# Weight sums in nine float32 tiles, GpSimd's sums in another order, sums of x split in three steps

## The chip, the cores and the metric

One core of a Trainium2 chip. The metric is the device time of one launch in microseconds. The program has five engines: TensorE (PE, matmuls), VectorE (DVE), ScalarE (ACT), GpSimd (POOL) and SyncE (SP), which only issues DMAs here.

## The reference

Two blocks of two layers each over 512 tokens of 1024 features in float32. The change lies in the feed-forward part of the second block, run twice:

```python
def squared_relu_mlp(x, w1, w2):
    h = jnp.square(jax.nn.relu(jnp.einsum('bsd,df->bsf', x, w1)))
    return jnp.einsum('bsf,fd->bsd', h, w2)

def second_block(x, mem, ...):
    for l in range(DEPTH):
        ...
        ff = squared_relu_mlp(x, w_ff1[l], w_ff2[l])
        x = layer_norm(ALPHA * x + ff, ln3_g[l], ln3_b[l])
    return x
```

w1 has 4096 columns (32 tiles of 128), w2 has 1024 (8 tiles). Everything ahead of it (attention, recurrence, gated feed-forward, memory attention) is computed as well and isn't touched.

## The kernel before, in words

A float32 matmul is made of three on float32r parts: each weight tile is split by ScalarE into a high part (`split_hi`, L1330) and by VectorE into the rest (`split_lo`, L1949), and TensorE adds high x high, low x high and high x low.

**Groups.** The 32 hidden tiles go in four groups of eight. The first group (f0 = 0) is an ordinary product. The other three (f0 = 8, 16, 24) use a scheme of Strassen's kind: two hidden tiles by the two halves of the 1024 inputs and the two halves of the 512 tokens make a pair, and a pair takes seven half-size products, the *forms*, in place of eight. A group has four pairs, 28 forms; form m = 7p + j is the j-th of pair p. Each has 12 matmuls of 256 columns on TensorE (`tensor_forms`, L1297 to L1302). After each group come the eight w_ff2 tiles w0 to w7, each 24 matmuls of 512 columns. So a layer runs: group 0, w0 to w7, then three times (28 forms, w0 to w7). With two layers there are six *form stages*, numbered 1 to 6 here.

**Weight sums.** The seven forms of a pair need sums of blocks of w_ff1. They are made by DMAs: SP loads a block of 256 KB into a half of a staging tile (*base load*, L2966), GpSimd issues further DMAs that add a block to it (L2885). A pair has four *chains*: chain 0 (forms 0 and, after one sum, 5), chain 1 (forms 1 and, after one, 4), chain 2 (form 2) and chain 3 (after two sums form 3, after the third form 6). *Sum (p,c,s)* is the s-th sum of chain c of pair p; a group has 20. A sum may only be issued once the chain's contents so far have been split for their form, and (p,3,s) once (p,3,s-1) has landed.

**Staging.** Three staging tiles of float32 hold all loaded weights. In a form stage they are six halves (`CHAIN_HALF`), so pair p+1's chains wait for pair p's splits. w0, w1 and w2 of the group can be loaded only after the splits of forms 27, 25 and 23 (`FORMS_STAGING`).

**Orders.** Every engine runs its list in order. ScalarE in `forms`: at each step m it waits for form m, at j = 0 copies `first` (L1870, needed by form j = 2 of that pair), at j = 1 `third` (needed by j = 5), at j = 2 the first result, then splits the high part of form m+6 (`split_form_hi`, L1337), and at j = 6 does relu, square and the high part of the hidden tile. VectorE follows with the low parts (`split_form_lo`, L1957) and the combinations (L2683 to L2701; L2687 is `inner2`, needed by j = 6). The splits of forms 0 and 1 come after w5's product, of 2 and 3 after w6's, of 4 and 5 after w7's. The split buffers (three) let form m+6 be split when form m is done.

GpSimd's order of a group before is (0,3,1), (0,3,2), then for p = 0 to 3: (p,0,1), (p,1,1), (p+1,3,1), (p,3,3), (p+1,3,2).

**Sums of x.** The forms also need sums of blocks of x (`sums`, L2661 to L2666, in temps 6 to 13), split into high parts by ScalarE (L1916) and low parts by VectorE (`sums_low`, L2672), the latter four at a time after the first four w_ff2 tiles of group 0.

## Time and profile before

| | us |
|---|---|
| median of 3 runs (2941.24 to 2949.04) | 2948.06 |
| the profiled execution | 2945.99 |
| its span, first to last instruction | 2944.3 |
| TensorE busy in the span | 2790.1 (95%) |
| VectorE, ScalarE, GpSimd busy | 1769.5, 1317.9, 508.7 |

The six form stages begin at 1793.28, 1892.83, 1997.48, 2619.05, 2725.42 and 2824.82 us of the span. Busy time of TensorE is modelled from pipelined matmuls; what counts is how far apart they start: 0.12 us for the forms' matmuls where nothing waits. In a view of windows the columns are: the stretch, its length in us, busy time (and instructions) of PE, PEld, DVE, ACT and POOL, the granted TensorE clock as a share of full speed, the busy share of the DMA engines, GB/s. An idle time in brackets ends when the named releaser's last semaphore event came; where that engine had waited itself, one reads on there.

### The profile page before, as it was taken

The page shows a single profiled execution, that of the slowest core. Times are in us where ns is not written, and L with a number is a line of the kernel's source. Part 1 is how long each engine was busy: PE and PEld are TensorE (multiplying, and loading weights), DVE is VectorE, ACT ScalarE, POOL GpSimd, SP SyncE. Part 2 cuts the span into 40 slices and gives each one's busy share as a digit, 9 for nine tenths or more (in the row PEclk, how much of TensorE's full clock was granted, in tenths as well). Part 3 has the DMA queues.
Part 4 walks back from the last instruction along what each step waited for, and adds up shares of the span by engine and source line. Part 5 has one row for each costly group of instructions (what it writes and reads, how often), then busy time and mean ns, then how long its engine had stood idle before and what let it go on. Part 6 is the DMA issues. An engine that isn't in the chain of part 4 may idle for free.

```text
span 2944.3 us, 41797 instructions
## 1 busy us (share of the span) xinstructions
PE 2790.1 (95%) x16644; PEld 2407.7 (82%) x16648; DVE 1769.5 (60%) x2793; ACT 1317.9 (45%) x2309; POOL 508.7 (17%) x425
## 2 busy tenths in 40 slices
...
GB/s 148 44 51 65 99 89 88 92 101 65 44 44 82 108 93 101 89 104 61 70 108 108 61 90 136 136 132 149 85 67 72 94 115 58 92 118 129 144 132 86
DMA packets 96129, 276.00 MB, mean 94 GB/s; under 512 B 11840, under 2 KB 13504, under 8 KB 95936
## 3 DMA queue, kind: packets, MB, share of 16 engines
...
## 4 chain that ended last, share of the span: by engine, by line
PE 76%; DVE 8%; DMA 6%; ACT 6%; issue 3%; POOL 0%; ACTq 0%; SPq 0%; DVEq 0%; POOLq 0%
PE psum L675 20%; PE psum L681 20%; PE psum L678 20%; DMA weights_float<-in_w_ff 6%; PE psum L747 2%; PE psum L770 1%; PE psum L774 1%; PE psum L772 1%; PE psum L1008 1%; PE psum L1036 1%; PE psum L1181 1%; ACT weights_hi_lo L1337 1%; PE psum L1193 1%; ACT weights_hi_lo L1330 1%; PE psum L1025 1%
## 5 line engine op out<-in xcount | busy, mean ns | idle before, releaser
L675 PE MATMUL psum<-act_hi_lo,weights_hi_lo 128*128 128x264 f32 (+2 forms) x2160 | 628.5, 337 | 3.7 <-ACT temp L1442 2.8
L1949 DVE TENSOR_TENSOR weights_hi_lo<-weights_float,weights_hi_lo 128x1024 fp32r<-128x1024 f32 (+1 forms) x384 | 481.6, 1255 | 221.9 <-ACT weights_hi_lo L1330 220.7
L1330 ACT ACTIVATE weights_hi_lo<-weights_float 128x1024 fp32r<-128x1024 f32 (+1 forms) x398 | 413.5, 1042 | 438.4 <-PE psum L681 336.3
L678 PE MATMUL psum<-act_hi_lo,weights_hi_lo 128*128 128x264 f32 (+2 forms) x2160 | 603.0, 325 | 1.9 <-DVE weights_hi_lo L1949 1.9
L681 PE MATMUL psum<-act_hi_lo,weights_hi_lo 128*128 128x264 f32 (+2 forms) x2160 | 604.0, 326 | 0.0
L675 PE MATMUL psum<-hidden_hi_lo,weights_hi_lo 128*128 128x512 f32 (+2 forms) x1584 | 519.5, 358 | 5.6 <-DVE temp L2698 1.6
L681 PE MATMUL psum<-hidden_hi_lo,weights_hi_lo 128*128 128x512 f32 (+2 forms) x1584 | 511.4, 353 | 1.5 <-DVE hidden_hi_lo L2220 1.4
L678 PE MATMUL psum<-hidden_hi_lo,weights_hi_lo 128*128 128x512 f32 (+2 forms) x1584 | 510.7, 352 | 1.3 <-DVE weights_hi_lo L1949 1.3
L675 PEld LDWEIGHTS psum<-act_hi_lo,weights_hi_lo 128*128 128x128 f32 x2160 | 369.1, 189 | 53.1 <-issue 17.7
L681 PEld LDWEIGHTS psum<-act_hi_lo,weights_hi_lo 128*128 128x128 f32 x2160 | 367.7, 189 | 33.0
L678 PEld LDWEIGHTS psum<-act_hi_lo,weights_hi_lo 128*128 128x128 f32 x2160 | 367.5, 189 | 33.1 <-issue 2.6
L675 PEld LDWEIGHTS psum<-hidden_hi_lo,weights_hi_lo 128*128 128x128 f32 x1584 | 279.8, 189 | 47.0 <-issue 3.0
L681 PEld LDWEIGHTS psum<-hidden_hi_lo,weights_hi_lo 128*128 128x128 f32 x1584 | 279.4, 189 | 42.9 <-DVE hidden_hi_lo L2220 2.0
L678 PEld LDWEIGHTS psum<-hidden_hi_lo,weights_hi_lo 128*128 128x128 f32 x1584 | 279.1, 188 | 40.4 <-DVE weights_hi_lo L1949 1.7
L2226 DVE SCALAR_TENSOR_TENSOR x_residual<-x_residual,psum 128x512 f32<-128x512 f32 (+1 forms) x108 | 74.6, 690 | 242.8 <-PE psum L681 242.8
L2885 POOL DMA_DIRECT2D weights_float<-in_w_ff x120 | 105.2, 930 | 601.2 <-DMA weights_float<-in_w_ff 464.1
L1337 ACT ACTIVATE weights_hi_lo<-weights_float 128x512 fp32r<-128x512 f32 x168 | 101.7, 626 | 215.0 <-DMA weights_float<-in_w_ff 134.0
L1957 DVE TENSOR_TENSOR weights_hi_lo<-weights_float,weights_hi_lo 128x512 fp32r<-128x512 f32 x168 | 114.5, 690 | 138.4 <-ACT weights_hi_lo L1337 136.9
L1297 PE MATMUL psum<-act_hi_lo,weights_hi_lo 128*128 128x256 f32 x288 | 91.2, 317 | 71.7 <-ACT arena L1870 63.8
L2780 POOL TENSOR_TENSOR temp<-temp 128x528 f32<-128x528 f32 (+1 forms) x28 | 43.6, 1555 | 479.3 <-ACT temp L1374 478.6
L1297 PEld LDWEIGHTS psum<-act_hi_lo,weights_hi_lo 128*128 128x128 f32 x288 | 60.8, 211 | 77.7 <-ACT arena L1870 67.8
L1551 ACT ACTIVATE hidden_hi_lo<-temp 128x528 fp32r<-128x528 f32 (+1 forms) x44 | 28.1, 639 | 201.7 <-DVE temp L2262 201.7
...
## 6 DMA issues: line engine op xcount, KB each, us to landing
...
weights_float<-in_w_ff POOLq DMA_DIRECT2D x120, 256.0 KB, 5.1
...
```

The costliest lines, as they stand in the source:

```text
L675: e.matmul(slot[:, place:place + c1 - c0], w_hi[:, col], x_hi[:, c0:c1], start=first, stop=False)
L678: e.matmul(slot[:, place:place + c1 - c0], w_lo[:, col], x_hi[:, c0:c1], start=False, stop=False)
L681: mm = e.matmul(slot[:, place:place + c1 - c0], w_hi[:, col], x_lo[:, c0:c1], start=False, stop=final)
L747: mm = e.matmul(slot[:, place:place + c1 - c0], weights, moving[:, c0:c1], start=first, stop=final)
L1297: e.matmul(K.bank[b][:, 0:HALF], w_hi[:, col], x_hi, start=not adds and k == 0, stop=False, skip_group_check=adds)
L1330: e.activation(K.parts(n)[0][:, 0:cols], K.staged(n)[:, 0:cols], ACT.Copy).then_inc(*K.did("hi", n))
L1337: e.activation(K.form_parts(l, f0, m)[0], K.chain(l, f0, p, FORM_CHAIN[j]), ACT.Copy).then_inc(*K.did("form_hi", l, f0, m))
L1949: e.tensor_tensor(lo[:, 0:cols], K.staged(n)[:, 0:cols], hi[:, 0:cols].bitcast(F32), ALU.subtract).then_inc(*K.did(name, n))
L1957: e.tensor_tensor(lo, K.chain(l, f0, p, FORM_CHAIN[j]), hi.bitcast(F32), ALU.subtract).then_inc(*K.did("form_lo", l, f0, m))
L2226: e.scalar_tensor_tensor(along(x, width), along(x, width), alpha, across(K.psum[slot], width), ALU.mult, ALU.add).then_inc(*K.did(*mark))
L2780: e.tensor_tensor(total, total, square[:, 0:width], ALU.add).then_inc(*K.did("square_sum", stage, l, k))
L2885: e.dma_start(K.chain(l, f0, p, chain), K.t["w_ff1"][l, f0 + 2 * p + tile, :, part * FORM:(part + 1) * FORM], accum_op=ALU.add).then_inc(* ...
```

## The change

- The four chains of a pair live in temps 5 to 13 (`CHAIN_TEMPS`): two tiles each for chains 0, 1 and 2, taken in turn, three for chain 3. A base load waits for the last split of the pair that had its tile before (`chain_before`), in the first group's first pairs for the last low part of the sums of x (`sum_lo`, 3, 3), as the sums of x lie in those temps.
- SP loads the chains of pairs 0 and 1 ahead of the load of w6 of the w_ff2 phase before the group, and those of pairs 2 and 3 after the load of w2 of the group itself. w0, w1 and w2 of the group no longer wait for the forms' splits, but for those of w7, w5 and w6 before them.
- GpSimd's order of a group: (0,3,1), (0,0,1), (0,1,1), (0,3,2), (1,3,1), (0,3,3), (1,3,2), (2,3,1), then for p = 1 to 3: (p,0,1), (p,1,1), (p,3,3), (p+1,3,2), (p+2,3,1).
- `sums_low` runs for k = 0, then 1 and 2, then 3 after w0, w1 and w2, in place of one after each of w0 to w3.

```diff
-CHAIN_HALF = ((0, 1, 2, 3), (4, 1, 2, 5))
+CHAIN_TEMPS = ((5, 6), (7, 8), (9, 10), (11, 12, 13))
...
+def chain_pair(f0, p):
+    return FORM_PAIRS * (f0 // (2 * FORM_PAIRS) - 1) + p
+
+
+def chain_temp(f0, p, chain):
+    return CHAIN_TEMPS[chain][chain_pair(f0, p) % len(CHAIN_TEMPS[chain])]
+
+
+def chain_before(f0, p, chain):
+
+
+    back = chain_pair(f0, p) - len(CHAIN_TEMPS[chain])
+    if back < 0:
+        return None
+    group, q = divmod(back, FORM_PAIRS)
+    return 2 * FORM_PAIRS * (group + 1), 7 * q + CHAIN_SPLITS[chain][-1]
...
-                if f0 == 0 and n < DC // 2:
-                    sums_low(n)
+                if f0 == 0 and n < 3:
+                    for k in ((0,), (1, 2), (3,))[n]:
+                        sums_low(k)
...
     long(0, 1)
-    long(0, 2)
     for p in range(FORM_PAIRS):
         split(7 * p)
         add(p, 0, 1, 1, 0)
         split(7 * p + 1)
         add(p, 1, 1, 1, 0)
-        long(p + 1, 1)
+        if p == 0:
+            long(0, 2)
+            long(1, 1)
         split(7 * p + 3)
         add(p, 3, 3, 0, 1)
         long(p + 1, 2)
+        long(p + 2, 1)
...
     def load(n):
-        after = K.after_forms(n)
-        if after is not None:
-            l, f0, i = after
-            w.wait_ge(*done("form_hi", l, f0, FORMS_STAGING[i]))
-            w.wait_ge(*done("form_lo", l, f0, FORMS_STAGING[i]))
-        elif n >= STAGING:
-            w.wait_ge(*done("hi", n - STAGING))
-            w.wait_ge(*K.low(n - STAGING))
+        before = n - STAGING
+        if before >= 0 and PIECES[before][0].startswith("forms"):
+            before -= STAGING
+        if before >= 0:
+            w.wait_ge(*done("hi", before))
+            w.wait_ge(*K.low(before))
...
+    def load_forms(l, f0, pairs):
+        for p in pairs:
             for chain in (0, 3, 2, 1):
-                half, before = K.chain_name(l, f0, p, chain), chain_before(p, chain)
+                before = chain_before(f0, p, chain)
                 if before is not None:
-                    w.wait_ge(*done("form_hi", l, f0, before))
-                    w.wait_ge(*done("form_lo", l, f0, before))
+                    w.wait_ge(*done("form_hi", l, *before))
+                    w.wait_ge(*done("form_lo", l, *before))
                 else:
-                    w.wait_ge(*done("hi", PIECE["forms", l, f0] - STAGING + half // 2))
-                    w.wait_ge(*K.low(PIECE["forms", l, f0] - STAGING + half // 2))
+                    w.wait_ge(*done("sum_lo", l, 3, DC // 2 - 1))
...
     for n in range(STAGING, len(PIECES)):
-        if PIECES[n][0] == "forms":
-            load_forms(*PIECES[n][1:])
-        elif PIECES[n][0] != "forms_end":
+        if n + 2 < len(PIECES) and PIECES[n + 2][0] == "forms":
+            load_forms(*PIECES[n + 2][1:], (0, 1))
+        name, l, *at = PIECES[n]
+        if not name.startswith("forms"):
             load(n)
+        if name == "w_ff2" and at[1] > 0 and at[0] == 2:
+            load_forms(l, at[1], (2, 3))
```

## Rows read from the trace of the kernel before

**Rows 1.** The page: the chain that ended last, by engine.

```profile
PE 76%; DVE 8%; DMA 6%; ACT 6%; issue 3%; POOL 0%; ACTq 0%; SPq 0%; DVEq 0%; POOLq 0%
```

**Rows 2.** TensorE's waits, whole span: total us, times, longest.

```profile
PE psum L1297 <- ACT arena L1870: 63.8, 20, 4.8
...
PE psum L1297 <- DVE arena L2687: 7.9, 8, 2.1
```

**Rows 3.** Windows (columns below), form 0 to w_ff2: stage 2, sum of six.

```profile
1892.83:1953.89 61.06, 47.10 (x338) 45.88 (x336) 31.76 (x56) 26.84 (x51) 14.95 (x17) 0.89 0.70 148
...
sum 348.94, PE 275.27 PEld 268.95 DVE 190.88 ACT 161.26 POOL 78.39; mean PE 45.88 PEld 44.83 DVE 31.81 ACT 26.88 POOL 13.07
```

**Rows 4.** Windows of six: forms 0-9, 9-16 (stage 3 too), 16-23, 23-w_ff2.

```profile
sum 117.26, PE 82.79 PEld 81.14 DVE 56.32 ACT 50.99 POOL 36.41; mean PE 13.80 PEld 13.52 DVE 9.39 ACT 8.50 POOL 6.07
...
2015.37:2028.89 13.52, 12.47 (x84) 12.27 (x84) 8.59 (x15) 7.15 (x14) 3.52 (x4) 0.82 0.80 169
...
sum 83.64, PE 74.32 PEld 73.10 DVE 51.51 ACT 43.00 POOL 24.01; mean PE 12.39 PEld 12.18 DVE 8.59 ACT 7.17 POOL 4.00
...
sum 85.84, PE 65.41 PEld 63.69 DVE 49.24 ACT 42.97 POOL 17.98; mean PE 10.90 PEld 10.62 DVE 8.21 ACT 7.16 POOL 3.00
...
sum 62.20, PE 52.76 PEld 51.02 DVE 33.80 ACT 24.30 POOL 0.00; mean PE 8.79 PEld 8.50 DVE 5.63 ACT 4.05 POOL 0.00
```

**Rows 5.** TensorE's timeline: forms 2, 9 (stage 2), end of 8, 9 (stage 3).

```profile
1899.54 0.39 PE L1297 MATMUL psum<-act_hi_lo,weights_hi_lo 128*128 128x256 f32 x1 [3.68 <-ACT arena L1870]
...
1916.02 0.58 PE L1297 MATMUL psum<-act_hi_lo,weights_hi_lo 128*128 128x256 f32 x1 [4.66 <-ACT arena L1870]
...
2010.32 0.28 PE L1302 MATMUL psum<-token_sums_hi_lo,weights_hi_lo 128*128 128x256 f32 x1
2015.37 0.58 PE L1297 MATMUL psum<-act_hi_lo,weights_hi_lo 128*128 128x256 f32 x1 [4.77 <-ACT arena L1870]
```

**Rows 6.** Timeline of ScalarE, stage 3: start, us, instruction, [idle before <-releaser].

```profile
1992.30 1.15 ACT L1337 ACTIVATE weights_hi_lo<-weights_float 128x512 fp32r<-128x512 f32 x2 [4.29 <-PE psum L681]
...
2012.05 1.15 ACT L1337 ACTIVATE weights_hi_lo<-weights_float 128x512 fp32r<-128x512 f32 x2 [6.54 <-DMA weights_float<-in_w_ff]
...
2014.95 0.37 ACT L1870 ACTIVATE arena<-psum 128x256 f32<-128x256 f32 x1
```

**Rows 7.** Timeline of GpSimd, stage 3: the issues of its sums.

```profile
1986.28 0.88 POOL L2885 DMA_DIRECT2D weights_float<-in_w_ff  x1 [3.45 <-DMA weights_float<-in_w_ff]
1988.82 0.87 POOL L2885 DMA_DIRECT2D weights_float<-in_w_ff  x1 [1.66 <-DVE weights_hi_lo L1957]
1991.28 1.75 POOL L2885 DMA_DIRECT2D weights_float<-in_w_ff  x2 [1.58 <-issue]
1994.96 0.88 POOL L2885 DMA_DIRECT2D weights_float<-in_w_ff  x1 [1.93 <-issue]
...
2004.62 1.86 POOL L2885 DMA_DIRECT2D weights_float<-in_w_ff  x2 [0.66 <-DVE weights_hi_lo L1957]
```

**Rows 8.** The chain that ended last, stages 2 and 3: start, us, what.

```profile
1895.79 5.94 DMA weights_float<-in_w_ff
...
1905.24 7.38 DMA weights_float<-in_w_ff
...
2004.62 7.35 DMA weights_float<-in_w_ff
```

**Rows 9.** Timelines of VectorE and ScalarE ahead of stage 1.

```profile
1774.01 1.42 DVE L2672 TENSOR_TENSOR token_sums_hi_lo<-temp,token_sums_hi_lo 128x256 fp32r<-128x256 f32 x4
...
1777.21 1.06 ACT L1330 ACTIVATE weights_hi_lo<-weights_float 128x1024 fp32r<-128x1024 f32 x1 [4.38 <-PE psum L681]
...
1782.66 0.63 ACT L1337 ACTIVATE weights_hi_lo<-weights_float 128x512 fp32r<-128x512 f32 x1 [4.38 <-PE psum L681]
```

**Rows 10.** Line 2966 on SP, 1779 to 1782 us: base loads, time to landing.

```profile
L2966 SPq DMA_DIRECT2D weights_float<-in_w_ff x4: 328/426/432, 1779.6 to 1780.9; - x4
...
DMA to landing us min/median/max: 5.5/5.9/6.1
```

More of the change, by code:

```diff
@@ L324 @@
 FORM_CHAIN = (0, 1, 2, 3, 1, 0, 3)
-CHAIN_HALF = ((0, 1, 2, 3), (4, 1, 2, 5))
+CHAIN_TEMPS = ((5, 6), (7, 8), (9, 10), (11, 12, 13))
 CHAIN_SPLITS = ((0, 5), (1, 4), (2,), (3, 6))
-CHAIN_SUMS = (1, 1, 0, 3)
 FORM_SUMS = (0, 0, 0, 2, 1, 1, 3)
-def chain_before(p, chain):
-    back = [q for q in range(p) if CHAIN_HALF[q % 2][chain] == CHAIN_HALF[p % 2][chain]]
-    return 7 * back[-1] + CHAIN_SPLITS[chain][-1] if back else None
+def chain_pair(f0, p):
[8 more added lines that the diff above has]
+    return 2 * FORM_PAIRS * (group + 1), 7 * q + CHAIN_SPLITS[chain][-1]
 FORMS_PARTS = [23, 25, 27]
-FORMS_STAGING = [27, 25, 23]
 def at_steps(table):
@@ L525, in chain @@
     def chain(self, l, f0, p, chain):
-        half = CHAIN_HALF[p % 2][chain]
-        return self.m["staging"][(PIECE["forms", l, f0] + half // 2) % STAGING][:, half % 2 * FORM:(half % 2 + 1) * FORM]
-    def chain_name(self, l, f0, p, chain):
-        half = CHAIN_HALF[p % 2][chain]
-        return half if half % 2 else 2 * ((PIECE["forms", l, f0] + half // 2) % STAGING)
+        return self.m["temps"][chain_temp(f0, p, chain)][:, 0:FORM]
     def form_parts(self, l, f0, m):
@@ L544, in form_there @@
         p, j = divmod(m, 7)
-        half = self.chain_name(l, f0, p, FORM_CHAIN[j])
+        chain = FORM_CHAIN[j]
+        temp = chain_temp(f0, p, chain)
         if FORM_SUMS[j] == 0:
-            return self.done(f"landed_chain{half}", l, f0, p, FORM_CHAIN[j])
-        return self.done(f"summed_chain{CHAIN_HALF[p % 2][FORM_CHAIN[j]]}", l, f0, p, FORM_CHAIN[j], FORM_SUMS[j])
+            return self.done(f"landed_chain{temp}", l, f0, p, chain)
+        return self.done(f"summed_chain{temp}", l, f0, p, chain, FORM_SUMS[j])
     def form_free(self, l, f0, m):
@@ L2883, in add @@
         if count > 1:
-            w.wait_ge(*done(f"summed_chain{CHAIN_HALF[p % 2][chain]}", l, f0, p, chain, count - 1))
+            w.wait_ge(*done(f"summed_chain{chain_temp(f0, p, chain)}", l, f0, p, chain, count - 1))
         e.dma_start(K.chain(l, f0, p, chain), K.t["w_ff1"][l, f0 + 2 * p + tile, :, part * FORM:(part + 1) * FORM],
-                    accum_op=ALU.add).then_inc(*did(f"summed_chain{CHAIN_HALF[p % 2][chain]}", l, f0, p, chain, count, by=16))
+                    accum_op=ALU.add).then_inc(*did(f"summed_chain{chain_temp(f0, p, chain)}", l, f0, p, chain, count, by=16))
     def split(m):
@@ L2893, in long @@
         if p < FORM_PAIRS:
[L2894 removed]
+            w.wait_ge(*done(f"landed_chain{chain_temp(f0, p, 3)}", l, f0, p, 3))
             add(p, 3, count, 1, count - 1)
     long(0, 1)
[L2898 removed]
     for p in range(FORM_PAIRS):
```

12 lines of the change are left out of this document (5 added, 7 removed).

## The prediction, made before the changed kernel was built

> **What bounds the kernel now.** I read the page first: TensorE is on 76% of the chain that ended last, and 6% of that chain, some 177 us, is DMA of the feed-forward weights [rows 1]. So TensorE sets the time except where weights come late, and only that share can be won by the change. The list of TensorE's waits says where: line 1297, the first matmul of a form, has the largest wait, 63.8 us in 20 waits, and 7.9 us more stand on a VectorE step there [rows 2]. All of this lies in the six form stages (three groups in each of two layers). The windows from form 0 to the first w_ff2 matmul give their sum, 348.9 us, 58.2 us on average, the second stage 61.1 [rows 3]. Without a wait a form takes 1.44 us (12 matmuls, 0.12 us apart), 28 take 40.3 us and six stages 242: **107 us are lost** there. No other stage is touched except the w_ff2 phase ahead of each group of forms.
>
> Four windows cut each stage at the forms that TensorE waits for (form 9, form 16, form 23); sums over six stages: 117.3, 83.6, 85.8 and 62.2 us, or 19.5, 13.9, 14.3 and 10.4 us a stage, against 13.0, 10.1, 10.1 and 7.2 us without waits [rows 4]. In stage 3 the wait ahead of form 9 is 4.8 us [rows 5], and behind it the granted clock averages 0.82 up to form 16: for part of that stretch TensorE has the lower of its two levels (1.2 of 2.4 GHz). Of the 13.5 us 12.5 are busy where seven forms need 10.1 [rows 4], so a long wait costs about 2.4 us more.
>
> What ends last at form 9? The wait is booked on ScalarE's copy L1870, but ScalarE itself had waited 6.54 us for a DMA before its split of form 11 and needed 3.3 us from there (split 11, split 12, the relu, square and high part, the copy) until form 9 began [rows 5, 6]. That DMA is sum (1,1,1): issued at 2004.6, landed 7.35 us later [rows 7, 8]. It waits for the split of form 8, which stands on ScalarE behind the split of form 6, and that one waits for sum (0,3,3). So the loop is: sum (0,3,3) lands, splits 6, 7 and 8, sum (1,1,1), splits 11 and 12, form 9. In stage 2 the chain shows it whole: sum (0,3,3) took 5.94 us to land, at 1901.7 or T+8.9, and the wait on sum (1,1,1) began 3.5 us later and took 7.38 us [rows 8]; form 9 began at T+23.2 [rows 5]. **The buffers are only half of this; the other half is a loop of DMA latencies that the change keeps.**
>
> **The change part by part.** I count from T, the start of form 0 (1997.48 in stage 3), and take stage 3 as the pattern.
>
> *More buffers, base loads earlier.* The loads of pairs 0 and 1 come before w6's load, some 40 us ahead of T (20 us in the first group of a layer). In stages 2 and 4 late base loads of pair 0 make form 2 wait, 3.7 us in stage 2 [rows 5]; this goes. The number of transfers is unchanged: 96 base loads, 120 sums.
>
> *Loads of w0 to w2 before the forms.* Their old waits for the splits of forms 23, 25 and 27 go; with them goes ScalarE's stop for w0 and what follows, the 7.9 us on L2687 [rows 2] and the stalls at the first w_ff2 tile. From form 23 on I put five forms, 7.2 us, and 0.9 for the low clock left by the wait at form 23: 8.1 in place of 10.4 us [rows 4]. **Gain 2.3 us a stage.**
>
> *GpSimd's order.* Before, sum (0,3,2) was issued at T-11.2, ahead of (0,0,1) at T-8.7 [rows 7]; split 3 ran at T-4.6 as the second of the pair at T-5.2 [rows 6], and (0,3,3) went out at T-2.5 [rows 7] and landed in time. Now (0,3,2) stands behind (0,0,1) at T-8.7 and (0,1,1) at T-7.8, so it goes out at T-6.9 as the third under way. Alone such a sum lands in 4.3 us (0.86 of issue and a wait of 3.45, [rows 7]); in company the rows have 5.9 to 7.4 us [rows 8]. I take 6.6: it lands at T-0.3. Split 3 follows, then VectorE's low part: (0,3,3) goes out at T+1.5 and lands, second under way, at about T+6.5. By the 3.5 us of stage 2, (1,1,1) goes out at T+10.0 (before: T+7.1), lands after 6.5 us (between 5.9 and 7.4 [rows 8], as fewer loads are about) at T+16.5, and form 9 begins 3.4 us on, at T+19.9. The mean before is 19.5 [rows 4]. **Loss 0.4 us a stage**: stage 2 had 23.2 and wins, stage 3 had 17.9 [rows 5] and loses 2. Ends: T+15 (every sum at 4.3 us) and T+23.7 (rival 3).
>
> *Sum (p+2,3,1) moved ahead of the next pair's splits.* It waits for a base load, and queued behind it on GpSimd are (p+1,0,1) and (p+1,1,1), for which ScalarE waits. For pair 2 SP is held by the split of form 5 (about T+2.2); its load lands by T+6.8, before split 7 is ready: hidden. For pair 3 SP's first load waits for split 12 (T+18.3), so (3,3,1) goes out at about T+22.4, just ahead of (2,0,1) and (2,1,1), and the latter becomes third under way. Form 9 to 16: 14.6 against 13.9 us. **Loss 0.7.** Form 16 to 23 then has neither such a sum nor loads under way; before, TensorE was busy for 10.9 of 14.3 us there [rows 4], and I leave it 2.5 us of waiting in place of 3.4. **Gain 0.9.**
>
> *Sums of x split sooner.* Four splits take 1.42 us and the last four ended at 1775.4 [rows 9]; behind the third tile they end a tile earlier (24 matmuls, 5.44 us between the two splits of rows 9) and one group of four later: about 1771.4. It must, as SP now waits for it, and behind SP's wait stand eight base loads and then w6 and w7. Eight issues at 0.43 us put w6's load at 1775. Loads issued beside a sum took 5.5 to 6.1 us [rows 10], so w6 lands at about 1781; its high part takes 1.06 us, VectorE's low part about as long, and TensorE wants both at 1782.5, when ScalarE's next wait for a product ends [rows 9]. Ends: 0 (it lands after 4 us) and 3 us. I take **1.5 us, twice** (first group of each layer). The eight small splits in a row on VectorE cost nothing: the next tile's product is awaited there anyway.
>
> Sum per stage: 2.3 - 0.4 - 0.7 + 0.9 = 2.1 us; six stages 12.6; less 3.0: **gain 9.6, say 10 us**. The profiled execution took 2946.0 us with a span of 2944.3; the median of the runs is 2948.06, 2.1 above it. 2936 us for a profiled execution, 2938 as a median.
>
> **The skill against it.** Base loads issued beside a sum landed in 5.5 to 6.1 us [rows 10]. The Trainium skill, DMA: Bandwidth & Descriptors, section "Issuing engines are not separate DMA queues", says that transfers issued by the sync and gpsimd engines run on the same 16 DMA engines and interleave. By it the early base loads hold up w6 in the first groups, and in exchange the sums in the forms lose company; the trace agrees in the first. What the second would give is rival 1.
>
> **Rivals.**
> 1. *Sums land sooner, because half the loads have left the form stage.* For it: the DMA share from form 9 to 16 is 0.80 [rows 4], and sums in company take long [rows 8]; against: three sums under way are company enough. If (0,3,2) takes 5.3, (0,3,3) 4.5, (1,1,1) 5.2, (2,1,1) 5.0 and (3,1,1) 1 us less, a stage gains 3.1 + 1.5 + 1.0 = 5.6 us, six 33: 2905 us in full, 2915 to 2930 in part.
> 2. *The fourth sum of a group waits as it does now.* Before, (0,1,1), the fourth, came out 1.6 us after GpSimd was free, 5.0 us after the issue of the second, (0,3,2), that is about when this landed [rows 7]; the other five stages look the same. Nothing in the code asks for it. Were (0,3,2), now the fourth, to wait for (0,0,1), it would go out at T-3.7; alone it then lands at T+1.5 and all that hangs on it moves 2 us: 12 us, **2950 us**.
> 3. *Slower.* One mechanism: (0,3,2) so late, by that wait and by company, that (0,3,3) lands at T+9 in every stage. Stage 2 is the sample: landed at T+8.9 [rows 8], form 9 at T+23.2 [rows 5]; with the latency of 7.4 us for (1,1,1) on top it would be some 0.5 later. With 23.7 in place of 19.9 six stages lose 23 us: **2961 us**. It passes 0.3% from form 9 at T+23.1.
> 4. *Little happens:* TensorE's waits merely change their name, 2944 us.
>
> **Chances.** Forecast 0.40, rival 1 0.22, rival 2 0.18, rival 3 0.15, rival 4 0.05. A measurement of this kernel tells about 0.3% (8.8 us) from no change, so the bounds are 2939.2 and 2956.9. The forecast stands beside the lower one: 0.24 of its 0.40 fall under it. Faster 0.24 + 0.22 = 0.46; slower 0.15 and some of rival 2, 0.18; the same 0.36. Range: all but the far end of rival 1 and of rival 3, 2912 to 2959. The forecast's own is 2930 to 2946.
>
> **What would show it.** Right: L1297 still has the largest wait, at form 9, with long rows of w_ff loads ahead of L1337; form 9 at T+19 to 21 in all six stages alike; no wait at form 2 or at form 27; w0's split at once after form 23; (0,3,2) out near T-6.9. A short wait of TensorE on w6 in the first groups. Wrong: form 9 at T+17 or sooner (rival 1), the sum out near T-3.7 (rival 2), or a wait of TensorE at forms 2 to 5 in each stage (rival 3).

## The result: slower by 0.24%, where a gain of 0.3% was forecast

The changed kernel takes 2952.85 us (median of 19 runs), the kernel before 2946.15 us (19 runs): ratio 1.0024, 95% interval 1.0017 to 1.0031. One run of the changed kernel took 3885.78 us at a granted clock of 0.65; it is not in the ratio, and the other 18 lie between 2946.65 and 2955.05. The forecast was 2938.0 us (2912 to 2959). The time lies in the range and the change is inside the 0.3% bound, but the sign was wrong: 7 us lost in place of 10 gained.

The profiled execution of the changed kernel has a span of 2950.8 us, 6.5 more than before. First the page: the chain that ended last, by engine, and then, from the waits of the whole span, the rows that answer to [rows 2] (total us, times, longest). All lines of the changed kernel are two further down: forms at L1299 to L1304, `first` at L1872, `split_form_hi` at L1339, `split_form_lo` at L1959, GpSimd's sums at L2888, base loads at L2968, `load` at L2956.

```profile
PE 74%; DVE 10%; ACT 6%; DMA 5%; issue 4%; POOL 1%; SPq 0%; ACTq 0%; DVEq 0%; POOLq 0%
...
PE psum L1299 <- ACT arena L1872: 67.1, 19, 6.7
PE psum L1299 <- DVE arena L2689: 5.6, 6, 1.6
...
PE psum L677 <- ACT weights_hi_lo L1332: 4.3, 4, 2.0
```

The forms' wait on `first` is not smaller but larger, 67.1 against 63.8 us, and its longest is 6.7 instead of 4.8 [rows 2]. The second row looks like the old 7.9 us, but it is another wait. In the kernel before it stood at form 27; there it is gone. Now it stands at form 6 in all six stages, 0.5 to 1.6 us. In stage 3:

```profile
2012.48 0.39 PE L1299 MATMUL psum<-act_hi_lo,weights_hi_lo 128*128 128x256 f32 x1 [0.70 <-DVE arena L2689]
```

VectorE's list has that step behind the low parts of forms 6 to 9, and the first of these waits for sum (0,3,3). In the kernels further down that have GpSimd's old order (e8, e6, e10, e11), form 6 has no such wait. Of the last row, the two long waits (1.6 and 2.0 us) are new: the first product on w6, in the first group of each layer, waits for its high part.

Next the windows (columns as told ahead of the prediction): the w_ff2 phase of the first group up to form 0, in both layers. The stretch begins at a short wait in an earlier product that both kernels have (1721.67 and 1723.97), 28.1 us ahead of w0's product. First the kernel before, then the changed one.

```profile
1721.67:1793.28 71.61, 71.61 (x383) 62.25 (x383) 51.75 (x85) 37.46 (x64) 5.41 (x6) 1.00 0.42 115
2547.44:2619.05 71.61, 71.59 (x383) 62.24 (x383) 51.16 (x84) 36.96 (x63) 2.69 (x3) 1.00 0.36 105
```

```profile
1723.97:1798.39 74.42, 72.13 (x382) 62.18 (x383) 50.79 (x84) 36.73 (x63) 3.72 (x4) 1.00 0.44 131
2552.42:2630.01 77.59, 75.02 (x383) 64.15 (x384) 50.75 (x85) 37.36 (x64) 4.45 (x5) 0.96 0.46 132
```

And the six form stages of the changed kernel, as sums over six: the whole stage, then forms 0 to 9, 9 to 16, 16 to 23, and 23 to the first w_ff2 product. They answer to [rows 3] and [rows 4].

```profile
sum 344.72, PE 269.77 PEld 263.59 DVE 193.15 ACT 159.70 POOL 80.24; mean PE 44.96 PEld 43.93 DVE 32.19 ACT 26.62 POOL 13.37
...
sum 124.86, PE 80.69 PEld 77.83 DVE 56.43 ACT 49.61 POOL 37.99; mean PE 13.45 PEld 12.97 DVE 9.40 ACT 8.27 POOL 6.33
...
sum 91.38, PE 72.65 PEld 71.44 DVE 51.46 ACT 43.23 POOL 26.49; mean PE 12.11 PEld 11.91 DVE 8.58 ACT 7.20 POOL 4.41
...
sum 79.36, PE 69.17 PEld 67.96 DVE 50.95 ACT 43.09 POOL 15.76; mean PE 11.53 PEld 11.33 DVE 8.49 ACT 7.18 POOL 2.63
...
sum 49.12, PE 47.25 PEld 46.37 DVE 34.31 ACT 23.77 POOL 0.00; mean PE 7.87 PEld 7.73 DVE 5.72 ACT 3.96 POOL 0.00
```

With these the whole difference can be booked, in us over the launch:

| part | forecast | measured (before, after) |
|---|---|---|
| end of a stage, form 23 to w_ff2 | gain 13.8 | gain 13.1 (62.20, 49.12) |
| form 16 to 23 | gain 5.4 | gain 6.5 (85.84, 79.36) |
| form 9 to 16 | loss 4.2 | loss 7.7 (83.64, 91.38) |
| forms 0 to 9 | loss 2.4 | loss 7.6 (117.26, 124.86) |
| w_ff2 phase of the first groups | loss 3.0 | loss 8.8 (143.22, 152.01) |
| start of the first phase (all that is upstream) | 0 | 2.3 later (1721.67, 1723.97) |
| sum | gain 9.6 | loss 6.8; the spans say 6.5 |

Both gains came as forecast. All three losses were forecast too small, by a factor of 1.8 to 3.2. The start of the first phase lies ahead of everything that the change touches; it varies by some us from one profiled execution to the next in all kernels here.

**Where form 9 waits.** Stage 3 of the changed kernel, T = 2002.99: GpSimd's timeline.

```profile
1994.38 2.68 POOL L2888 DMA_DIRECT2D temp<-in_w_ff  x3 [25.35 <-DVE weights_hi_lo L1959]
1998.88 0.86 POOL L2888 DMA_DIRECT2D temp<-in_w_ff  x1 [1.83 <-issue]
2003.92 1.79 POOL L2888 DMA_DIRECT2D temp<-in_w_ff  x2 [4.17 <-ACT weights_hi_lo L1339]
2012.79 2.66 POOL L2888 DMA_DIRECT2D temp<-in_w_ff  x3 [7.08 <-DMA temp<-in_w_ff]
...
2027.52 2.68 POOL L2888 DMA_DIRECT2D temp<-in_w_ff  x3 [7.63 <-DMA temp<-in_w_ff]
```

By the order of its list these are (0,0,1), (0,1,1), (0,3,2); then (1,3,1); then (0,3,3) and (1,3,2); then (2,3,1), (1,0,1), (1,1,1). GpSimd stood 7.08 us at (2,3,1) for a DMA, and (1,1,1), the sum that form 9 hangs on, was third behind it. The DMA is the base load of pair 2's chain 3. SP's rows for the four loads of that pair:

```profile
L2968 SPq DMA_DIRECT2D temp<-in_w_ff x4: 327/456/490, 2005.3 to 2006.7; - x4
...
DMA to landing us min/median/max: 5.0/6.9/8.6
```

They were issued at T+2.3 to T+3.7, just behind (0,3,3) and (1,3,2) (2003.9 and 2004.8), and took up to 8.6 us. Chain 3's is the second of them and landed at T+9.4. ScalarE, for which GpSimd no longer waits there, was ready long before:

```profile
2008.22 0.63 ACT L1339 ACTIVATE weights_hi_lo<-temp 128x512 fp32r<-128x512 f32 x1 [3.21 <-DMA temp<-in_w_ff]
...
2009.81 1.15 ACT L1339 ACTIVATE weights_hi_lo<-temp 128x512 fp32r<-128x512 f32 x2
...
2020.17 1.15 ACT L1339 ACTIVATE weights_hi_lo<-temp 128x512 fp32r<-128x512 f32 x2 [7.27 <-DMA temp<-in_w_ff]
```

Split 6 at 2008.2 shows (0,3,3) landed at T+5.2, sooner than forecast (T+6.5); splits 7 and 8 were done by about 2011, T+8. The last row is the wait for (1,1,1). The chain that ended last tells the same story, first for stage 3, then (ahead of it in time) for w6 and the first sums of stage 1:

```profile
2003.92 1.79 POOL temp L2888 x2
2005.71 7.07 issue
2012.79 1.15 POOL temp L2888 x2
2013.94 6.14 DMA temp<-in_w_ff
```

```profile
1778.15 8.92 DMA weights_float<-in_w_ff
...
1792.30 9.26 DMA temp<-in_w_ff
...
1822.20 0.58 PE psum L1299
```

Stage 1 lost most: form 9 at T+23.8 (1822.20), before T+17.3. Its first sums went out at 1791.2, right behind SP's loads of w0, w1 and w2 (1789.5 to 1790.3), which had been held back by the late w6 and w7; the third of them took 9.26 us. Form 2 waited 2.15 us in this stage, which it had not done before.

### The profile page after: what moved, and what is told of

Its sections match the earlier page's. It is cut to its first block, busy times and chain, and to the rows that moved or that the text cites. A ratio compares the mean times of both kernels' runs of the same rounds, so it can differ in the third digit from the quotient of the medians.

```text
span 2950.8 us, 41741 instructions
## 1 busy us (share of the span) xinstructions
PE 2791.0 (95%) x16648; PEld 2405.8 (82%) x16648; DVE 1769.9 (60%) x2793; ACT 1316.3 (45%) x2309; POOL 509.6 (17%) x425
## 4 chain that ended last, share of the span: by engine, by line
PE 74%; DVE 10%; ACT 6%; DMA 5%; issue 4%; POOL 1%; SPq 0%; ACTq 0%; DVEq 0%; POOLq 0%
PE psum L677 19%; PE psum L683 19%; PE psum L680 19%; DMA temp<-in_w_ff 4%; PE psum L749 2%; PE psum L1299 1%; PE psum L772 1%; PE psum L776 1%; PE psum L774 1%; PE psum L1010 1%; PE psum L1302 1%; DVE weights_hi_lo L1951 1%; PE psum L1304 1%; PE psum L1183 1%; PE psum L1195 1%
## 5 line engine op out<-in xcount | busy, mean ns | idle before, releaser
L677 PEld LDWEIGHTS psum<-act_hi_lo,weights_hi_lo 128*128 128x128 f32 x2160 | 368.7, 189 | 53.3 <-issue 17.7
L2888 POOL DMA_DIRECT2D temp<-in_w_ff x120 | 106.1, 1033 | 610.1 <-DMA temp<-in_w_ff 340.7
L1959 DVE TENSOR_TENSOR weights_hi_lo<-temp,weights_hi_lo 128x512 fp32r<-128x512 f32 x168 | 114.7, 690 | 149.8 <-ACT weights_hi_lo L1339 148.2
L1339 ACT ACTIVATE weights_hi_lo<-temp 128x512 fp32r<-128x512 f32 x168 | 101.4, 626 | 217.8 <-DMA temp<-in_w_ff 142.6
L1299 PE MATMUL psum<-act_hi_lo,weights_hi_lo 128*128 128x256 f32 x288 | 90.0, 312 | 72.7 <-ACT arena L1872 67.1
L1299 PEld LDWEIGHTS psum<-act_hi_lo,weights_hi_lo 128*128 128x128 f32 x288 | 60.2, 209 | 78.0 <-ACT arena L1872 71.0
L1553 ACT ACTIVATE hidden_hi_lo<-temp 128x528 fp32r<-128x528 f32 (+1 forms) x44 | 28.1, 639 | 202.7 <-DVE temp L2264 202.7
```

The lines of the kernel that those rows point to most:

```text
L677: e.matmul(slot[:, place:place + c1 - c0], w_hi[:, col], x_hi[:, c0:c1], start=first, stop=False)
L1299: e.matmul(K.bank[b][:, 0:HALF], w_hi[:, col], x_hi, start=not adds and k == 0, stop=False, skip_group_check=adds)
L1339: e.activation(K.form_parts(l, f0, m)[0], K.chain(l, f0, p, FORM_CHAIN[j]), ACT.Copy).then_inc(*K.did("form_hi", l, f0, m))
L1959: e.tensor_tensor(lo, K.chain(l, f0, p, FORM_CHAIN[j]), hi.bitcast(F32), ALU.subtract).then_inc(*K.did("form_lo", l, f0, m))
L2888: e.dma_start(K.chain(l, f0, p, chain), K.t["w_ff1"][l, f0 + 2 * p + tile, :, part * FORM:(part + 1) * FORM], accum_op=ALU.add).then_inc(* ...
```

## The experiments

Offsets are from T, the start of form 0, as means over the six stages of one profiled execution; the last column is the sum of the six windows from form 0 to the first w_ff2 product. "Ratio" is against the kernel before on the same chip.

| kernel | median us | ratio, 95% | form 9 | 9-16 | 16-23 | 23-end | sum |
|---|---|---|---|---|---|---|---|
| before | 2946.15 | | 19.5 | 13.9 | 14.3 | 10.4 | 348.9 |
| the change | 2952.85 | 1.0024 (1.0017-1.0031) | 20.8 | 15.2 | 13.2 | 8.2 | 344.7 |
| e1_w6_first | 2934.66 | 0.9958 (0.9946-0.9971) | 20.0 | 15.4 | 13.7 | 8.0 | 342.9 |
| e2_base_sum_later | 2930.83 | 0.9945 (0.9924-0.9965) | 18.6 | 13.4 | 13.2 | 9.4 | 327.2 |
| e3_chain3_first | 2929.18 | 0.9945 (0.9926-0.9965) | 18.9 | 13.5 | 13.0 | 8.7 | 324.5 |
| e4_second_sum_early | 2929.93 | 0.9955 (0.9940-0.9969) | 17.7 | 14.9 | 13.1 | 7.7 | 320.8 |
| e8_old_order | 2912.41 | 0.9883 (0.9862-0.9903) | 16.3 | 13.7 | 13.4 | 8.0 | 308.3 |
| e6_all_a | 2908.52 | 0.9865 (0.9844-0.9886) | 15.9 | 13.5 | 13.3 | 9.1 | 310.4 |
| e7_all_b | 2911.52 | 0.9882 (0.9861-0.9903) | 16.7 | 13.3 | 13.2 | 8.7 | 311.8 |
| b1_late32 | 2962.62 | 1.0052 (1.0034-1.0071) | 21.8 | 14.3 | 14.5 | 10.2 | 364.2 |
| e10_old_order_w0_late | 2924.33 | 0.9914 (0.9886-0.9942) | 15.6 | 13.4 | 13.1 | 10.4 | 315.4 |
| e9_w0_late | 2970.10 | 1.0066 (1.0044-1.0089) | 20.4 | 15.4 | 13.4 | 10.8 | 359.9 |
| e5_ring | 2956.46 | 1.0036 (1.0022-1.0050) | 21.8 | 15.0 | 13.0 | 8.2 | 347.7 |
| e11_all_a_ring | 2899.92 | 0.9836 (0.9820-0.9852) | 15.3 | 13.3 | 13.1 | 8.9 | 303.4 |

**First round: each suspect alone, on the changed kernel.** The theory was that the sum (2,3,1), waiting for its base load, holds up (1,1,1); the rival that the late (0,3,2) does.

*w6 ahead of the base loads in the first groups.*

```diff
-        if n + 2 < len(PIECES) and PIECES[n + 2][0] == "forms":
+        if n + 2 < len(PIECES) and PIECES[n + 2][0] == "forms" and PIECES[n + 2][2] > FF2_FIRST[1]:
             load_forms(*PIECES[n + 2][1:], (0, 1))
...
             load(n)
+        if n + 1 < len(PIECES) and PIECES[n + 1][0] == "forms" and PIECES[n + 1][2] == FF2_FIRST[1]:
+            load_forms(*PIECES[n + 1][1:], (0, 1))
```

In the first form group of a layer alone, the base loads of pairs 0 and 1 go out behind the load of w7 instead of ahead of that of w6.

> The changed kernel, but in the first group of each layer SP issues the loads of w6 and w7 ahead of the eight base loads. Theory: in the changed kernel w6 landed 8 us after its issue behind eight base loads, TensorE lost 2.8 us in layer 0 and 6.0 us in layer 1 there, and the delay of w6 and w7 pushed the loads of w0 to w2 into the company of the first three sums of stage 1 (8 to 9 us to land), which cost 3 us more at form 9. All of it goes: 10 to 12 us less than the changed kernel, 2941 to 2943 us. Rival: the base loads come later by as much, the first sums with them, and the gain is given back in stages 1 and 4: 2950 to 2953 us.

Measured 2934.66 us. Windows of the two phases, same stretch as above:

```profile
1717.82:1789.43 71.61, 71.59 (x382) 62.26 (x383) 51.07 (x84) 36.91 (x63) 4.59 (x5) 1.00 0.49 143
2542.92:2614.53 71.61, 71.60 (x383) 62.26 (x383) 51.14 (x85) 37.52 (x64) 4.45 (x5) 1.00 0.48 143
```

Both are back at 71.61 us: the loss of 8.8 us is all due to the order on SP. Stage 1's form 9 comes at T+21.8 in place of T+23.8, so the stages give 1.8 more. That is 10.6 us, what the theory said; the medians say 18, and the intervals of the two kernels don't allow less than some 13 (0.9971 against 1.0017). Between the two profiled executions another 6.1 us lie ahead of the first phase (1717.8 against 1724.0), where both run the same program. I have no cause for it and leave it open.

*(p+2,3,1) back behind the next pair's (p,0,1) and (p,1,1).*

```diff
-        if p == 0:
-            long(0, 2)
-            long(1, 1)
+        if p == 0:
+            long(0, 2)
+        long(p + 1, 1)
         split(7 * p + 3)
         add(p, 3, 3, 0, 1)
         long(p + 1, 2)
-        long(p + 2, 1)
```

> The changed kernel with sum (p+2,3,1) put back behind (p+1,1,1) in GpSimd's order. Theory A: at form 9 GpSimd stands at sum (2,3,1), which waits for its base load until T+9.5, and (1,1,1) is behind it; with the order back, (1,1,1) goes out at about T+8.4 in place of T+10.9 and form 9 begins at about T+18 in place of T+20.5: six stages, 12 to 15 us less than the changed kernel, about 2939 us. Theory B, that of the prediction: the loop from sum (0,3,2) over (0,3,3) to split 8 sets form 9, and (2,3,1) is hidden: form 9 stays within 0.5 us, 2950 to 2953 us.

2930.83 us, and GpSimd in stage 3 (T = 1991.70):

```profile
1993.00 1.78 POOL L2888 DMA_DIRECT2D temp<-in_w_ff  x2 [4.23 <-ACT weights_hi_lo L1339]
1999.66 2.65 POOL L2888 DMA_DIRECT2D temp<-in_w_ff  x3 [4.88 <-ACT weights_hi_lo L1339]
```

(0,3,3) goes out at T+1.3 as in the change; but the row of three is now (1,0,1), (1,1,1), (2,3,1) and waits for ScalarE's splits, not for a DMA. (1,1,1), its second, goes out near T+8.8 in place of T+10.9; form 9 gains 2.2 us a stage, form 9 to 16 1.9; the end of a stage takes 1.2 us longer. The theory gave form 9 rightly; that the same stop costs pair 3 as much is the second half of the gain, and so it is 22 us where 12 to 15 were expected.

*The stop kept, but its load first.*

```diff
-            for chain in (0, 3, 2, 1):
+            for chain in (0, 3, 2, 1) if p < 2 else (3, 0, 2, 1):
```

> The changed kernel with GpSimd's order as it is, but SP loads chain 3 of pairs 2 and 3 ahead of chain 0, so that it does not stand behind chain 0's wait for the splits of forms 5 and 12. Theory A: base load (2,3) then lands some 10 us before T, (2,3,1) does not wait, form 9 begins 2 to 2.6 us sooner in each stage, form 16 up to 1 us sooner: 13 to 18 us less than the changed kernel, 2935 to 2940 us. Theory B: no change at form 9, 2950 to 2953 us.

2929.18 us, the same as the move of the sum gave. Chain 3 has three tiles, so its load for pair 2 has no split of this stage to wait for; in the change it stood on SP behind chain 0's load, which waits for the split of form 5. Put first it goes out 15 us sooner, at T-12.4 in place of T+2.7, and lands 5.6 us later (T = 1994.93):

```profile
1982.58 15.97 SPq L2968 DMA_DIRECT2D temp<-in_w_ff  x4
```

(The row takes in the three loads that follow when the wait is over.) So it is the landing of that one load, and nothing else about (2,3,1), that cost.

*(0,3,2) back ahead of (0,0,1).*

```diff
     long(0, 1)
+    long(0, 2)
     for p in range(FORM_PAIRS):
...
         if p == 0:
-            long(0, 2)
             long(1, 1)
```

> The changed kernel with sum (0,3,2) put back to the second place of GpSimd's order. Theory A: (0,3,3) lands earlier by 3 us, but (1,1,1) still waits behind (2,3,1), whose base load waits for the split of form 5; that split comes only some 0.5 us sooner at most: 0 to 4 us less than the changed kernel. Theory B: form 9 begins 3 us sooner in each stage, 18 us less, 2935 us.

2929.93 us: the rival was right as well. Form 9 comes 3.1 us sooner although (2,3,1) is still in its place. GpSimd and SP's loads of pair 2 in stage 3 (T = 1991.03):

```profile
1964.21 0.88 POOL L2888 DMA_DIRECT2D temp<-in_w_ff  x1 [6.47 <-DMA temp<-in_w_ff]
1982.42 2.68 POOL L2888 DMA_DIRECT2D temp<-in_w_ff  x3 [17.32 <-DVE weights_hi_lo L1959]
1988.46 0.88 POOL L2888 DMA_DIRECT2D temp<-in_w_ff  x1 [3.36 <-issue]
...
1997.22 2.65 POOL L2888 DMA_DIRECT2D temp<-in_w_ff  x3 [6.25 <-DVE weights_hi_lo L1959]
```

```profile
L2968 SPq DMA_DIRECT2D temp<-in_w_ff x4: 328/432/486, 1993.3 to 1994.7; - x4
...
DMA to landing us min/median/max: 2.8/3.3/3.6
```

With the new tiles (0,3,1) and (0,3,2) can go out as soon as their base load has landed: (0,3,2) at 1964.2, **T-26.8**. In the kernel before it was T-11.2 [rows 7], in the changed kernel T-6.8. Then (0,3,3) goes out at T-2.6, and when SP issues pair 2's loads at T+2.3 one sum is under way, (1,3,2): they land in 2.8 to 3.6 us instead of 5.0 to 8.6. So (2,3,1), (1,0,1), (1,1,1) go out from T+6.2, and the stop at the base load has nearly gone too. One early sum removed both, except at pair 3 (form 9 to 16 still 14.9 us).

**Second round: both together, and the order alone on the old kernel.** *GpSimd's whole old order in the changed kernel* (the edits of e2 and e4).

> The change's buffers, loads and splits with GpSimd's order of the kernel before: sum (0,3,2) ahead of (0,0,1) again, and (p+2,3,1) no longer ahead of the next pair's splits. Theory A (both halves of the new order cost, one behind the other: the late (0,3,2) starts the loop late, (2,3,1) then holds GpSimd for a base load; each alone gave some 21 us): together form 9 at T+16.5 to T+17.5 in all six stages, form 9 to 16 in 13.4 us, form 16 to 23 in 13.2, the end in 8.2, so 51.5 us a stage, 309 in all against 321 and 327 with one of them: 2914 to 2920 us. Theory B (one limit, reached by either edit; what is left is the latency of the sums themselves): no more than the single edits, 2926 to 2931 us, the stages' sum still 320 to 325.

2912.41 us, stages' sum 308.3, form 9 at 16.3: the first theory within 2 us. Stage 3 (T = 1983.62), GpSimd and SP's loads of pair 2:

```profile
1956.69 0.88 POOL L2888 DMA_DIRECT2D temp<-in_w_ff  x1 [6.75 <-DMA temp<-in_w_ff]
1974.95 2.73 POOL L2888 DMA_DIRECT2D temp<-in_w_ff  x3 [17.38 <-DVE weights_hi_lo L1959]
1981.04 0.88 POOL L2888 DMA_DIRECT2D temp<-in_w_ff  x1 [3.36 <-issue]
...
1990.31 1.77 POOL L2888 DMA_DIRECT2D temp<-in_w_ff  x2 [0.42 <-ACT weights_hi_lo L1339]
```

(0,3,3) is the row at 1981.04 (T-2.6) and (1,1,1) leads the row at 1990.31, **T+6.7**. Forms 0 to 9 take 97.87 us in all six stages together, 27.0 us less than in the change. **The new order of GpSimd's sums costs 40 us; everything else in the change gains 34.** (2952.9, 2912.4 and 2946.2 us; by the ratios, each against the kernel before on its own chip, 41 and 34.)

*The same with w6 first* (the edit of e1), and *with chain 3's load first in place of the moved sum* (e1, e3 and e4).

> The kernel with GpSimd's old order and, besides, w6 of the first group loaded ahead of the base loads of the group that follows. Theory A: the w_ff2 phases of the first groups lose their waits on w6 (2 and 6 us against the kernel before), the first stage no longer has its loads of w0 to w2 beside its first sums: 6 to 10 us less than the kernel with the old order alone, 2905 to 2912 us. Theory B: the base loads of the first two pairs, now later, miss the splits of forms 0 to 3 in stages 1 and 4, and the gain of the phase is lost there: the same time as without the edit.

> The new place of (p+2,3,1) kept, but (0,3,2) ahead of (0,0,1), chain 3 first among the base loads of pairs 2 and 3, and w6 first as above. Theory A (what holds GpSimd at (2,3,1) is the time at which its base load lands, and no more than that): form 9 at T+17, form 9 to 16 in 13.5 to 14 us, sum of the stages 310 to 315, 2908 to 2916 us, level with the kernel that moves the sum. Theory B (three sums under way is the limit, so a sum of chain 3 ahead of (p,0,1) and (p,1,1) costs a place in any case): (1,1,1) goes out 1 to 3 us later than there, form 9 at T+18 to 19, 2918 to 2926 us.

2908.52 and 2911.52 us, against 2912.41 without w6 first: intervals that overlap, where 6 to 10 us were expected. The waits of the first groups are nearly gone. This is their row in the kernel with the old order alone, then in the one with w6 first:

```profile
PE psum L677 <- ACT weights_hi_lo L1332: 4.7, 4, 2.2
```

```profile
PE psum L677 <- ACT weights_hi_lo L1332: 0.7, 2, 0.5
```

The stages' sum is 2.1 us higher in its profiled execution (310.4). By the medians some 4 us are left of the gain, which is inside the noise, so what w6 first is worth here isn't shown. The two ways round (2,3,1) end level again: the landing of its load was the only thing about it.

*One part alone on the kernel before: (0,3,2) behind (0,0,1) and (0,1,1).*

```diff
     long(0, 1)
-    long(0, 2)
     for p in range(FORM_PAIRS):
...
         add(p, 1, 1, 1, 0)
+        if p == 0:
+            long(0, 2)
         long(p + 1, 1)
```

> The kernel before with one part of the change alone: sum (0,3,2) moved behind (0,0,1) and (0,1,1), everything else as before. Theory A (the loop of (0,3,2), (0,3,3), (1,1,1) sets form 9, so its later start is paid in full): (0,3,2) goes out at T-7 in place of T-11, form 9 is 2 to 3 us later in the stages where base loads don't hold it anyway, 8 to 16 us in all: 2954 to 2962 us. Theory B (form 9 is set by the late base loads of the staging halves; the loop has slack in the kernel before): within 4 us of the kernel before, 2942 to 2950 us.

2962.62 us, 15 more than before: the theory's upper end. GpSimd in stage 3 (T = 2003.73):

```profile
1995.07 2.68 POOL L2885 DMA_DIRECT2D weights_float<-in_w_ff  x3 [4.95 <-DVE weights_hi_lo L1957]
...
2004.96 0.88 POOL L2885 DMA_DIRECT2D weights_float<-in_w_ff  x1 [4.71 <-ACT weights_hi_lo L1337]
```

(0,3,2) goes out as third at T-6.9 and (0,3,3) at T+1.2 instead of T-2.5: the 3.7 us later start of the loop gives form 9 at 21.8 against 19.5. It isn't paid in full, but in all six stages.

**Third round: the early loads of w0 to w2, and the room for GpSimd's DMAs.** In the next two w0, w1 and w2 wait again for the splits of forms 27, 25 and 23; the loads of pairs 2 and 3 go ahead of them.

```diff
+        after = K.after_forms(n)
+        if after is not None:
+            l, f0, i = after
+            w.wait_ge(*done("form_hi", l, f0, (27, 25, 23)[i]))
+            w.wait_ge(*done("form_lo", l, f0, (27, 25, 23)[i]))
-        if before >= 0:
+        elif before >= 0:
...
+        if name == "w_ff2" and at[1] > 0 and at[0] == 0:
+            load_forms(l, at[1], (2, 3))
         if not name.startswith("forms"):
             load(n)
-        if name == "w_ff2" and at[1] > 0 and at[0] == 2:
-            load_forms(l, at[1], (2, 3))
```

> The kernel with the change's tiles and GpSimd's old order (2912.4 us), but w0, w1 and w2 of a group wait again for the splits of forms 27, 25 and 23. Theory A (the early loads are worth what the windows of the end of the stage say, 8.2 against 10.4 us): form 23 to the first w_ff2 product takes about 10.4 us again, everything ahead of it stays: 13 us more, 2923 to 2928 us. Theory B (the wait at the end of a stage is cover for something that is late anyway, or the early loads delay the first sums as much as they bring): within 4 us of 2912.

> The changed kernel with that same edit: w0, w1 and w2 wait for the splits of forms 27, 25 and 23. Theory A: the end of the stage is 2.2 us longer, but stage 1 is relieved of the three loads that land beside its first sums (form 9 at T+20 in place of T+23.8), so 8 to 11 us more than the changed kernel, 2960 to 2964 us. Theory B (loads of w0 to w2 don't matter to the sums of stage 1): 13 us more, 2966 us, form 9 of stage 1 still at T+23 to 24.

On the old order 2924.33 us, 12 more, and the sum over six of form 23 to the first w_ff2 product is back where the kernel before had it [rows 4]:

```profile
sum 62.46, PE 51.49 PEld 49.75 DVE 33.36 ACT 25.00 POOL 0.00; mean PE 8.58 PEld 8.29 DVE 5.56 ACT 4.17 POOL 0.00
```

On the changed kernel 2970.10 us, 17 more by medians and more than either theory gave. Form 9 of stage 1 comes at T+21.1 in place of T+23.8, near what the first theory said of the collision (on the old order it comes at T+15.6 in place of T+18.8). The price for the end of a stage, 2.2 us, was too low: 2.6 in this kernel. And the four w_ff2 phases between stages take 180.1 us in place of 174.5, with no wait in them, at a granted clock of 0.95 to 0.98; no theory had this term.

*Room for GpSimd's DMAs.* All kernels so far show rows of at most three sums.

```diff
-LINE_PAD = 96
+LINE_PAD = 16
...
-... dynamic_dma_scratch_size=1024)
+... dynamic_dma_scratch_size=1536)
```

> The changed kernel with room for half as many descriptors again for GpSimd's DMAs (1536 in place of 1024 bytes a partition; paid for by 80 columns less of one small tile). In every kernel so far GpSimd has issued at most three sums before the first of them had landed, though nothing in the program asks for it. Theory A (the limit is that room): four or more sums are issued in one row without a pause, (1,3,1) directly behind (0,3,2), 2.5 us sooner. The time changes little, as (0,3,2) isn't held up in the changed kernel: 2948 to 2956 us, since sums in company land later. Theory B (the limit lies elsewhere): still x3 and a pause of 1.6 to 2 us; time as the changed kernel within 3 us.

```profile
1990.47 3.54 POOL L2888 DMA_DIRECT2D temp<-in_w_ff  x4 [25.52 <-DVE weights_hi_lo L1959]
...
2008.71 3.56 POOL L2888 DMA_DIRECT2D temp<-in_w_ff  x4 [6.32 <-DMA temp<-in_w_ff]
```

Rows of four, (1,3,1) directly behind (0,3,2) (T = 1999.03): the room was the limit. The time, ratio 1.0036 against 1.0024 with overlapping intervals, doesn't gain by it: the second row again waits at (2,3,1) until T+9.7, and form 9 is 1.0 us a stage later in this execution.

> The fastest kernel so far (GpSimd's old order, w6 of the first group first; 2908.5 us) with room for four of GpSimd's sums. There the fourth sum of a stage, (1,3,1), comes out 3.4 us after GpSimd is free, held by nothing but that room. Theory A (sums are limited by places): (1,3,1) goes out directly behind (0,1,1), about 3 us sooner, its successors (1,3,2) and (1,3,3) follow, and form 9 to 16 loses some of its wait: 0.5 to 1.5 us a stage, 2899 to 2906 us. Theory B (sums are limited by the transfers themselves; a fourth one under way only makes the other three land later, (0,3,2) among them, which is the head of the loop): row of four, but form 9 unchanged or up to 1 us later, 2906 to 2915 us.

2899.92 us, the fastest kernel here, 1.6% below the kernel before. The number is that of the first theory, but its mechanism isn't: I had taken the fourth sum of a stage there for (1,3,1), held by the room. GpSimd's rows say otherwise (T = 1981.50):

```profile
1972.79 2.76 POOL L2888 DMA_DIRECT2D temp<-in_w_ff  x3 [17.39 <-DVE weights_hi_lo L1959]
1978.89 0.88 POOL L2888 DMA_DIRECT2D temp<-in_w_ff  x1 [3.34 <-issue]
...
1990.88 0.89 POOL L2888 DMA_DIRECT2D temp<-in_w_ff  x1 [0.83 <-issue]
```

The pause of 3.3 us is still there. In the old order the row of three is (0,0,1), (0,1,1), (1,3,1), and the fourth is (0,3,3), which by the code waits for the split of form 3, and that stands behind w6's product. The larger room does show later: the last row is (1,3,3), out at T+9.4 with three sums still under way, where without it this sum came at T+10.1 (1996.20, T = 1986.07), just after the first of the three had landed. But 0.6 of the gain of 1.2 us a stage is there at form 9 already, ahead of anything that this sum can move. So where the 7 us between the stages' sums (310.4, 303.4) come from isn't settled; the two kernels ran on different chips, and their intervals overlap.

## Why the prediction was wrong

**Where the kernel is bound: right.** The forms' wait, the loop (0,3,3), splits 6 to 8, (1,1,1), splits 11 and 12, form 9, is what these kernels move along, but in the changed kernel (1,1,1) waited for the load ahead of it and not for split 8. T+1.5 for (0,3,3) was T+0.9; it went out at T+1.2 in the one-part kernel, where form 9 moved with it. No wait at form 2 in stages 2 and 4, none at form 27: right. Not foreseen: 2.15 us at form 2 in stage 1, and the waits at form 6, 5.6 us in all.

**End of the stage and form 16 to 23: right**, 13.1 and 6.5 us against 13.8 and 5.4, the first confirmed by taking it out of the kernel with the old order (12 us).

**Rival 2 (the fourth sum waits): fell in its form.** (0,3,2), fourth of the stage, stands in a row of three with no pause (1994.38). What waits is the fourth of those under way, (1,3,1), and the larger room shows why. The pause of [rows 7] ended, as I had read it, when (0,3,2) landed (1990.95, the next sum at 1991.28; in stage 1 1788.27 and 1788.52), but only two sums were under way there. So the room isn't a plain count of three; what rule it follows isn't shown.

**Two steps failed: sum (p+2,3,1) "hidden", and w6 at 1.5 us a layer.** Against the forecast the time is 16.4 us over (9.6 gained, 6.8 lost). By the table above 5.8 of these stand on w6 and 5.2 on forms 0 to 9, of which 3.9 are stage 1, where the loads held back by w6 and w7 met the first sums. 3.5 stand on form 9 to 16, the stop at (3,3,1), and 2.3 lie upstream. With w6 first (e1) the kernel is 0.4% faster than before, where the whole change was forecast at 0.3%; part of that is the difference ahead of the first phase that I can't explain. The stop at (2,3,1) takes more off the clock than its share of the miss, 22 us (e2): (0,3,3) landed 1.3 us sooner than forecast in stage 3, so part of the stop is covered when one counts against the forecast.

**Sum (p+2,3,1) "hidden".** The load was to land by T+6.8; it landed at T+9.4. I had counted SP's wait (T+2.2, measured T+2.3) and then a load of 4.6 us, without asking which sums GpSimd would have just issued: (0,3,3) and (1,3,2), 0.5 to 1.4 us before. Beside them the four loads took 5.0 to 8.6 us. My own rows had 5.5 to 6.1 us for base loads beside one sum [rows 10], and I used them for w6 only. So (1,1,1) went out at T+10.9, though (0,3,3) had landed 1.3 us sooner than forecast; without the stop it is T+8.8 (e2). For pair 3 I had (3,3,1) at T+22.4; it was T+24.5 (2027.52), again at a base load's landing, and form 9 to 16 took 15.2 instead of 14.6 us; without the stop 13.4. There no company was to blame: the four loads landed in 2.7 to 4.3 us, but SP issued them at T+20.3, not at T+18.3, as form 9 was late.

**Forms 0 to 9: 20.8 against 19.9.** 0.9 us a stage of which stage 1 alone, with T+23.8, makes 0.65. That collision of w0 to w2 with the first sums, 2.0 us by e1, 2.7 by e9 and 3.2 by e10 against e8, had no term in the forecast.

**The order priced against the wrong kernel.** I set the new place of (0,3,2), T-6.9 (measured T-6.8), against the old T-11.2 and found a small loss, since stages 2 and 4 gain by their base loads. But that old time was itself due to the late base loads that the new tiles remove. The change thus gave up T-26.8, and with it 3.1 us (e4 against the change) or 2.3 us (e8 against e2) of the 4.5 between 20.8 and 16.3. The sentence that the change "keeps" the loop hid this: the tiles free its head, and only the order ties it again. The time forecast didn't need this step, but the judgement of rivals did: the time of rival 1 (sums land sooner, form 9 early; 2905 us in full, 2915 to 2930 in part) is near what the kernel takes with the old order, 2912 us; with the change's order no stage shows it.

**w6 late: right mechanism, a third of the size.** Its load was forecast to be issued at 1775 and went out at 1777.7; 2.3 of that are upstream's. But beside eight base loads it took 7.6 us, and w7's 8.9, where I had put 6:

```profile
L2956 SPq DMA_DIRECT2D weights_float<-in_w_ff x2: 375/484/592, 1777.7 to 1778.2; - x2
...
DMA to landing us min/median/max: 7.6/8.2/8.9
```

```profile
1786.45 0.47 PE L677 MATMUL psum<-hidden_hi_lo,weights_hi_lo 128*128 128x512 f32 x1 [1.59 <-ACT weights_hi_lo L1332]
1787.62 0.50 PE L680 MATMUL psum<-hidden_hi_lo,weights_hi_lo 128*128 128x512 f32 x1 [0.70 <-DVE weights_hi_lo L1951]
```

2.3 us here for w6 and 2.8 in all in layer 0; in layer 1 6.0, as the granted clock fell to 0.96 over the phase too. The Trainium skill, DMA: Bandwidth & Descriptors, section "Issuing engines are not separate DMA queues", says transfers that SP and GpSimd issue share the 16 DMA engines and interleave. The trace agrees: loads beside two sums took 5.0 to 8.6 us, the same loads with one sum under way 2.8 to 3.6. The misses at w6, at pair 2's load and in stage 1 are cases of that rule, which I quoted and then followed for one term of three; the late issue of pair 3's loads and the price of the order are not.
